# Strassen's algorithm on pairs of column tiles in three feed-forward products of a float32 kernel

## The chip, the cores and the metric

The kernel runs on one core of a Trainium2 chip. The metric is the device time of one execution in microseconds (us). All data are float32.

## The reference

Two transformer blocks run one after the other over 512 tokens of width 1024. The first is attention, convolution and gated linear attention, then a feed-forward network, then a per-layer gate. The second is a Fourier mixer beside an RWKV mixer, then a feed-forward network with a 3x3 convolution in its middle. What matters here are the two feed-forward networks, with 2816 hidden columns each:

```python
# first block
h = rms_norm(x, ffn_norm_g[i])
x = x + (jax.nn.silu(h @ ffn_w_gate[i]) * (h @ ffn_w_up[i])) @ ffn_w_down[i]
gate = jax.nn.sigmoid(rms_norm(x, ple_norm_g[i]) @ ple_w_gate[i])
x = x + (p[i] @ ple_w_proj[i]) * gate
...
# second block
x = x + g2 * conv_ffn(h, ffn_w_up[l], ffn_conv_w[l], ffn_conv_b[l], ffn_w_down[l], rows)
# conv_ffn: depthwise 3x3 convolution of h @ w_up, then (silu(gate) * val) @ w_down
```

## The kernel before

Activations lie transposed: 128 channels on the partitions, 512 tokens along the row. A weight matrix comes as a stream of **units** of 512 KB, each eight 128x128 tiles. A unit is the eight contraction tiles of one 128-column tile. SyncE loads the units in the order of `STREAM` into a ring of four slots and reloads a slot when `units_done` says that TensorE has finished with it. `product` (L330 is its matmul) multiplies the eight tiles of a unit with the eight token tiles of 512 columns and accumulates them in one PSUM bank.

Every engine has its own queue, written out by hand, stage after stage, and the engines meet only at semaphores. The parts that the change touches come in this order on TensorE:

- `out1` (L1205): eight units; VectorE adds each result to the residual stream `xT` (L1232).
- `norm_ffn`: ScalarE scales and squares each `xT` tile as it comes (L369, L370), GpSimd adds the squares (L386), TensorE sums over partitions with a matrix of ones (L394, L396), ScalarE takes the root (L374, L375, each behind a table load). It is folded: the products run on values that are not yet divided by the root, and VectorE multiplies the results by it.
- `ffn1` (L330): 22 pairs of a gate unit and an up unit. VectorE rescales both (L1314, L1316), ScalarE takes the silu (L1298), VectorE multiplies (L1319). Between the units lie 28 units of another product, `ada` (L1155), that is not part of the network.
- `ple_project` (L1345): two units, with ScalarE copying the results out (L1356).
- `down1` (L1205): 24 units, 22 contraction tiles for each of eight output tiles, with 12 more `ada` units between.
- `norm_ple` and `ple_gate` (L330 again): the same folded norm, and eight units.
- much later `ffn2` (L330): 44 units. ScalarE copies each result into a padded grid (L2547), VectorE applies nine taps to it (L2576, L2578), ScalarE takes the silu (L2554), VectorE multiplies (L2587).
- `down2` (L1205): 24 units, VectorE adding with a gate factor (L1234), then the last norm (L394, L396, L374, L375, L408) and the stores.

In `ffn2` and in a few other stages TensorE walks through its units in a hardware loop of four units; in `ffn1` and `down1` they are written out.

## Time and profile before

| what | value |
|---|---|
| median of three runs | 1976.53 us (1972.60 to 1979.27) |
| span of the profiled execution | 1970.1 us; its own time is not listed apart from these three |
| what lies around the span | 2.5 to 9.2 us by the three runs, 6.4 us by the median |
| TensorE busy | 1876.9 us, 95% of the span |
| VectorE, ScalarE, GpSimd busy | 770.6, 477.2, 237.2 us |
| mean granted TensorE clock | 0.985 |

The span runs from the first to the last instruction. Each matmul of the program shows as two rows of the trace, and so does each weight load, so a unit of eight matmuls is 16 rows.

### The profile page before, as it was taken

How to read it: one execution, taken by the hardware profiler on the slowest of the kernel's cores; microseconds unless marked ns; L12 is line 12 of the kernel's file. 1: busy time of each engine (PE TensorE's matmuls, PEld its weight loads, DVE VectorE, ACT ScalarE, POOL GpSimd, SP SyncE). 2: the span in 40 equal slices, each digit the busy share in tenths (PEclk: the TensorE clock that was granted, in tenths of full speed). 3: DMA queues.
4: the chain of work that ended last, by engine and by line, in shares of the span. 5: the costliest groups of instructions: out<-in, count | busy, mean ns of one | idle time of the engine just before them, and what ended most of it. 6: DMA issues, size and time to landing. Idle time of an engine off the chain costs nothing.

```text
span 1970.1 us, 33620 instructions
## 1 busy us (share of the span) xinstructions
PE 1876.9 (95%) x13862; PEld 995.4 (51%) x13862; DVE 770.6 (39%) x1560; ACT 477.2 (24%) x982; POOL 237.2 (12%) x284
## 2 busy tenths in 40 slices
PE   7999999999999999999999979888898999999997
PEld 3455774444444444434455448888743444444443
DVE  3551451011111100003332367666634888898001
ACT  3022562210000000033411554444412222221001
POOL 1140011000000000013000045555110000000000
PEclk9999998999999999999999989999999999999999
DMA  6421001333432223333311200000111222222222
GB/s 225 155 76 60 37 1 64 107 129 130 148 129 78 82 92 122 117 118 129 142 54 54 70 1 5 5 4 4 52 54 64 75 75 75 81 79 75 75 85 96
DMA packets 43862, 158.63 MB, mean 81 GB/s; under 512 B 5017, under 2 KB 5673, under 8 KB 42713
## 3 DMA queue, kind: packets, MB, share of 16 engines
q1 hardware_dynamic: 37440, 133.19, 20.0%
q10 hardware_dynamic: 6296, 23.58, 3.3%
q8 instruction: 102, 1.67, 0.4%
q14 instruction: 24, 0.19, 0.0%
HBM read 152.01 MB, written 6.31 MB: 80 GB/s over the span
## 4 chain that ended last, share of the span: by engine, by line
PE 88%; DVE 5%; ACT 4%; issue 1%; DMA 0%; POOL 0%; DVEq 0%; SPq 0%; ACTq 0%; POOLq 0%
PE psum L330 47%; PE psum L1205 21%; PE psum L1987 2%; PE psum L1991 2%; PE psum L995 1%; DVE mem L2177 1%; PE psum L588 1%; PE psum L1155 1%; PE psum L976 1%; PE psum L963 1%; PE psum L1753 1%; PE psum L631 1%; PE psum L1345 1%; PE psum L1998 1%; DVE mem L2205 1%
## 5 line engine op out<-in xcount | busy, mean ns | idle before, releaser
L330 PE MATMUL psum<-mem 128*128 128x512 f32 (+1 forms) x2272 | 961.5, 582 | 19.9 <-DMA mem<-in_units 11.7
L330 PEld LDWEIGHTS psum<-mem 128*128 128x128 f32 x2272 | 426.9, 190 | 525.0 <-issue 509.8
L1205 PE MATMUL psum<-mem 128*128 128x512 f32 x960 | 420.0, 596 | 4.1 <-DVE mem L2497 2.6
L1205 PEld LDWEIGHTS psum<-mem 128*128 128x128 f32 x960 | 181.3, 190 | 235.0 <-issue 227.3
L2578 DVE SCALAR_TENSOR_TENSOR mem<-mem 128x512 f32<-128x512 f32 x352 | 235.0, 744 | 0.0
L386 POOL TENSOR_TENSOR mem<-mem 128x512 f32<-128x512 f32 x24 | 30.5, 1270 | 1094.2 <-ACT mem L370 1093.8
L1987 PE MATMUL psum<-mem 64*64 64x64 f32 x1920 | 73.8, 222 | 12.1 <-DVE mem L2205 5.4
L1298 ACT ACTIVATE mem<-mem 128x512 f32<-128x512 f32 x22 | 13.9, 630 | 290.7 <-DVE mem L1314 290.6
L1234 DVE SCALAR_TENSOR_TENSOR mem<-psum,mem 128x512 f32 x16 | 12.0, 750 | 177.4 <-PE psum L1205 177.4
L1991 PE MATMUL psum<-mem 64*64 64x64 f32 x1920 | 71.4, 221 | 2.5 <-issue 2.0
L1987 PEld LDWEIGHTS psum<-mem 64*64 64x64 f32 x1920 | 64.7, 136 | 17.7 <-DVE mem L2205 10.9
L1316 DVE TENSOR_TENSOR mem<-psum,mem 128x512 f32<-128x512 f32 x22 | 15.2, 692 | 144.1 <-PE psum L330 144.1
L1225 DVE TENSOR_TENSOR mem<-mem,psum 128x512 f32<-128x512 f32 x8 | 5.5, 688 | 168.4 <-PE psum L1205 168.4
L1314 DVE TENSOR_TENSOR mem<-psum,mem 128x512 f32<-128x512 f32 x22 | 15.2, 692 | 138.8 <-PE psum L330 128.4
L2547 ACT COPY mem<-psum 128x512 f32<-128x512 f32 x44 | 25.8, 587 | 174.6 <-PE psum L330 174.5
L1991 PEld LDWEIGHTS psum<-mem 64*64 64x64 f32 x1920 | 64.0, 135 | 5.1 <-issue 3.3
L370 ACT ACTIVATE mem<-mem 128x512 f32<-128x512 f32 x32 | 19.9, 623 | 192.5 <-DVE mem L1234 192.5
L2294 ACT COPY mem<-psum 128x256 f32<-128x256 f32 x120 | 45.0, 375 | 88.2 <-PE psum L1987 86.7
L2204 DVE COPY_PREDICATED mem<-mem,psum 128x256 f32<-128x256 int32 x96 | 40.9, 426 | 35.3 <-PE psum L1991 35.2
L1035 DVE CUSTOM_DVE_ANT_0 mem<-psum,mem 128x512 f32<-128x512 f32 (+3 forms) x64 | 28.9, 489 | 46.2 <-PE psum L963 46.2
L2143 POOL TENSOR_TENSOR mem<-mem 128x256 f32<-128x256 f32 x12 | 12.0, 998 | 269.4 <-DVE mem L2160 269.4
L2205 DVE STREAM_TRANSPOSE mem<-mem 128x256 f32<-128x256 f32 x96 | 42.8, 446 | 3.3
(355 smaller groups left out, 1743.8 us busy)
## 6 DMA issues: line engine op xcount, KB each, us to landing
mem<-in_units SPq DMA_DIRECT2D x248, 512.0 KB, 3.4
mem<-in_cw ACTq DMA_DIRECT2D x2, 2048.0 KB, 10.4
mem<-in_wn ACTq DMA_DIRECT2D x1, 2048.0 KB, 8.6
bias_tiles<-bias_scratch ACTq DMA_DIRECT2D x1, 2048.0 KB
mem<-bias_tiles ACTq DMA_DIRECT2D x1, 2048.0 KB, 10.5
mem<-in_xT ACTq DMA_DIRECT2D x1, 2048.0 KB, 9.9
x_scratch<-mem ACTq DMA_DIRECT2D x1, 2048.0 KB, 8.7
mem<-x_scratch ACTq DMA_DIRECT2D x1, 2048.0 KB, 8.2
```

The costliest lines, as they stand in the source:

```text
L330: last = pe.matmul(dst, ring[:, slot, k, :], rhs(k), start=(k == 0), stop=(k == 7))
L370: eng.activation(sqr[:, k, 0:n], src(k), ACT.Square).then_inc(squared, 1)
L386: steps.link(eng.tensor_tensor(sqr[:, 0, 0:n], sqr[:, 0, 0:n], sqr[:, k, 0:n], ALU.add))
L1035: last = eng.tensor_tensor_reduce(sc[u % 2][g][:, 0:n], bank[:, 0:n], bias[:, h, 128 * (3 - i):512], -1.0, 1e20, ALU.add, ALU.min, low[u % ...
L1205: last = eng.matmul(ps[m % 4], ring[:, slot, k - 8 * part, :], rhs(k), start=(k == 0), stop=(k == ktiles - 1))
L1987: each(lambda hp, c, t: eng.matmul(dst(E_[d], hp, t), g[t, hp, 1, :], T[t, hp, :], start=True, stop=True)).then_inc(q["made"], 1)
L1991: each(lambda hp, c, t: eng.matmul(dst(O_[d], hp, t), a[t, hp, :], b_[t, hp, :], start=True, stop=True)).then_inc(q["made"], 1)
L2204: steps.link(eng.copy_predicated(split(T), bc22(kept), heads(O_[d])))
L2205: eng.transpose(flat(Tt), flat(T)).then_inc(q["grown"], 1)
L2294: eng.copy(split(s["Z"]), heads(E_[d])).then_inc(q["kept"], 1)
L2547: eng.copy(pad[:, j, 1:9, 1:65], ps[j].rearrange("p (y x) -> p y x", y=8)).then_inc(padded, 1)
L2578: steps.did_but(1, lambda: eng.scalar_tensor_tensor(cacc[:, j], src, w, cacc[:, j], ALU.mult, ALU.add))
```

## The change

`ffn1`, `down1` and `down2` no longer multiply one column tile at a time. They take **two column tiles at once**, halve the contraction and the tokens (512 into 256 and 256), and form the 2x2 block product with seven half-width products instead of eight, in the variant of the algorithm that shares sums. A product of `ffn1` has four contraction tiles (`half`), one of `down1` and `down2` has eleven, taken in chunks of four, four and three (`CHUNKS`, `part`).

- **Weight sums.** VectorE forms four sums of weight tiles for each pair of units, `lay_weights` and `lay_last_weights`, each 128x512 (128x384 for the last chunk): 22 times in `ffn1`, 12 times in each `down`. The pair of units for the next step is summed during the current one.
- **Token sums.** For `ffn1` VectorE forms them tile by tile behind `out1` (`lay_tokens`: one operation of 128x256 for each of the first four tiles, three for each of the last four). For `down1` and `down2` GpSimd forms them (`lay_products`), four operations of 128x256 for each of 11 pairs of hidden tiles.
- **PSUM partial results.** In `ffn1` ScalarE copies one bank out three times in a step (`head`, `mid`, `tail`), because four products accumulate in it one behind the other, and VectorE adds these copies to two other banks. The order on TensorE in step n is p11(n), p22(n-1), the `ada` units, s1(n), s4(n-1), s2(n), p12(n), s3(n). In the `down` products 11 half-width VectorE operations for each pair of output tiles take the place of two full-width ones, and ScalarE copies one half bank.
- **Order.** `ple_project` moves from before `down1` to after it, its two units on either side of the norm's sum; the norms take their tiles in the order 0, 4, 1, 5, 2, 6, 3, 7. The `ada` units are grouped: two in each of the first six steps, one in each of the other 16.
- **Ring and loops.** From `ffn1` to `ple` the ring has six slots. TensorE's and SyncE's loops over units are written out everywhere.

```diff
-STREAM = [("in1", 17), ("out1", 8), ("ffn1", 2 * FT + 28), ("pleproj", 2), ("down1", 36),
+STREAM = [("in1", 17), ("out1", 8), ("ffn1", 2 * FT + 28), ("down1", 36), ("pleproj", 2),
           ("ple", 16), ("in2", 19), ("out2", 8), ("ffn2", 2 * FT), ("down2", 24)]
+WIDE = ("ffn1", "down1", "pleproj", "ple")
+NSLOTS, NWIDE = 4, 6
...
+    for _ in range(_c):
+        _s = min(range(NWIDE if _n in WIDE else NSLOTS), key=lambda k: _last[k])
+        _turns[_s] += 1
+        SLOT.append(_s)
+        TURN.append(_turns[_s])
...
+        _last[_s] = NUNITS
+        NUNITS += 1
+HALF = FT // 2
+CHUNKS = [(0, 4), (4, 8), (8, 11)]
...
+        def lay_weights(eng, done, base, w1, w2, to, nk):
+            at = (slice(None), slice(0, nk), slice(None))
+            hi = (slice(None), slice(4, 4 + nk), slice(None))
+            eng.tensor_tensor(to[:, 0][at], w2[at], w2[hi], ALU.add).then_inc(done, 1)
+            eng.tensor_tensor(to[:, 2][at], w1[at], w2[at], ALU.subtract).then_inc(done, 1)
+            eng.wait_ge(done, base + 1)
+            eng.tensor_tensor(to[:, 1][at], to[:, 0][at], w1[at], ALU.subtract).then_inc(done, 1)
...
+            at = (slice(None), slice(0, nk), slice(None))
+            eng.wait_ge(done, base + 3)
+            eng.tensor_tensor(to[:, 3][at], w1[:, 4:4 + nk, :], to[:, 1][at], ALU.subtract).then_inc(done, 1)
...
+        def lay_products(eng, base, lo, hi, to):
+            eng.tensor_tensor(to[:, 0], lo[:, CTX:S], lo[:, 0:CTX], ALU.subtract).then_inc(act_laid, 1)
+            eng.wait_ge(act_laid, base + 1)
+            eng.tensor_tensor(to[:, 1], hi[:, CTX:S], to[:, 0], ALU.subtract).then_inc(act_laid, 1)
+            eng.tensor_tensor(lo[:, CTX:S], hi[:, CTX:S], lo[:, CTX:S], ALU.subtract).then_inc(act_laid, 1)
+            eng.wait_ge(act_laid, base + 2)
+            eng.tensor_tensor(to[:, 2], hi[:, 0:CTX], to[:, 1], ALU.subtract).then_inc(act_laid, 1)
...
+                def half(dst, w, rhs, start=True, stop=True, before=None):
+                    for k in range(4):
+                        if before:
+                            before(k)
+                        last = eng.matmul(dst, w[:, k, :], rhs(k), start=start and k == 0, stop=stop and k == 3,
+                                          skip_group_check=True)
+                    return last
...
+                for n in range(FT):
+                    p11(n)
+                    if n:
+                        p22(n - 1)
+                    else:
+                        s1(n)
+                        sums(eng, steps)
+                        eng.wait_ge(cond, 1)
+                    ada_units(eng, sum(ADA1[:n]), ADA1[n])
+                    if n == 6:
                         ctx_sum(eng)
+                    if n:
+                        s1(n)
+                        s4(n - 1)
+                    s2(n)
+                    p12(n)
+                    s3(n)
+                p22(FT - 1)
+                s4(FT - 1)
...
+                    eng.wait_ge(made, after("11", n))
+                    if n:
+                        eng.wait_ge(taken, 4 * (n - 1) + 1)
+                    eng.copy(head, bank_y(n)).then_inc(kept, 1)
...
+                    eng.wait_ge(made, after("s2", n))
+                    if n:
+                        eng.wait_ge(taken, 4 * (n - 1) + 4)
+                    eng.copy(mid, bank_y(n)).then_inc(kept, 1)
+                    if n % 2:
+                        q = n // 2
+                        for side in (1, 0):
+                            eng.wait_ge(taken, 4 * (n - 1) + 3)
+                            eng.wait_ge(scaled, 2 * n - side)
+                            g = actT[:, q + HALF * side, :]
+                            eng.activation(g, g, ACT.Silu).then_inc(silued, 1)
+                    eng.wait_ge(units_done, pair_unit(n) + 1)
+                    if n:
+                        eng.wait_ge(taken, 4 * (n - 1) + 2)
+                    eng.copy(tail, bank_y(n)).then_inc(kept, 1)
...
+                    if n:
+                        eng.wait_ge(kept, 3 * m + 3)
+                        eng.wait_ge(made, after("s1", m))
+                        eng.tensor_tensor(place(m, 1)[:, CTX:S], bank_z(m), tail, ALU.add).then_inc(taken, 1)
+                        eng.wait_ge(units_done, pair_unit(m) + 2)
+                        if m == 0:
+                            rooted(eng)
+                        eng.tensor_tensor(place(m, 1)[:, 0:CTX], bank_y(m), rstd[:, 0:CTX], ALU.mult).then_inc(taken, 1)
+                        scale(place(m, 1)[:, CTX:S], rstd[:, CTX:S], m, 4 * m + 2)
+                        if n == FT:
+                            down1_first[0](eng)
+                        eng.wait_ge(made, after("s4", m))
+                        eng.tensor_tensor(place(m, 0)[:, CTX:S], bank_z(m), mid, ALU.add).then_inc(taken, 1)
+                        scale(place(m, 0), rstd, m, 4 * m + 4)
+                    if n + 1 < FT:
+                        pair_sums(eng, n + 1)
+                        pair_last_sum(eng, n + 1)
+                    if n and m % 2:
+                        q = m // 2
+                        eng.wait_ge(taken, 4 * m + 3)
+                        for side in (1, 0):
+                            eng.wait_ge(silued, 2 * q + 2 - side)
+                            eng.wait_ge(scaled, 2 * m + 2 - side)
+                            g = actT[:, q + HALF * side, :]
+                            eng.tensor_tensor(g, g, upT[:, side, :], ALU.mult).then_inc(multiplied, 1)
...
+                    if n < FT:
+                        eng.wait_ge(made, after("12", n))
+                        eng.wait_ge(kept, 3 * n + 1)
+                        eng.tensor_tensor(place(n, 0)[:, 0:CTX], bank_x, head, ALU.add).then_inc(taken, 1)
+            def pool(eng, steps):
+                for q in range(HALF):
+                    eng.wait_ge(multiplied, 2 * q + 2)
+                    lay_products(eng, 4 * q, actT[:, q, :], actT[:, q + HALF, :], actX[:, :, q, :])
...
+                        return ins
+                    def freed(count):
...
+                    if between:
+                        between(eng, j)
+                    if m == 0:
+                        eng.wait_ge(act_laid, laid + 4 * k1)
+                    unit_landed(eng, u)
+                    freed(2)
+                    if first and m:
+                        eng.wait_ge(kept, r + m)
+                    part(a[:, lo], held(u), lambda k: low(k)[:, lo], True, False)
+                    ins = part(a[:, hi], held(u)[:, 4:8], lambda k: high(k)[:, lo], False, True)
+                    if last_:
+                        ins.then_inc(made, 1)
+                    freed(4)
+                    eng.wait_ge(summed, s0 + 4 * j + 3)
+                    part(b[:, lo], to[:, 1], lambda k: extras[:, 1, k, :], True, False)
+                    ins = part(b[:, hi], to[:, 2], lambda k: low(k)[:, hi], False, True)
+                    if last_:
+                        ins.then_inc(made, 1)
+                    freed(10)
+                    eng.wait_ge(summed, s0 + 4 * j + 4)
+                    part(c[:, lo], to[:, 0], lambda k: extras[:, 0, k, :], True, False).then_inc(units_done, 1)
+                    ins = part(c[:, hi], to[:, 3], lambda k: high(k)[:, hi], False, True)
+                    if last_:
+                        ins.then_inc(made, 1)
+                    freed(11)
+                    unit_landed(eng, u + 1)
+                    part(d[:, lo], held(u + 1)[:, 4:8], lambda k: extras[:, 2, k, :], True, True).then_inc(units_done, 1)
...
+                        weights(eng, j + 1)
+                        continue
+                    m = j // 3
+                    t = 11 * (r + m)
+                    x, y = xT[:, m, :], xT[:, m + 4, :]
+                    eng.wait_ge(made, 3 * (r + m) + 1)
+                    eng.wait_ge(kept, r + m + 1)
+                    add(x[:, lo], a[:, lo], m)
+                    eng.wait_ge(taken, t + 1)
+                    add(x[:, lo], a[:, hi], m)
+                    if j < 11:
+                        weights(eng, j + 1)
+                    eng.wait_ge(made, 3 * (r + m) + 2)
+                    eng.tensor_tensor(u2, b[:, lo], p1, ALU.add).then_inc(taken, 1)
+                    eng.wait_ge(taken, t + 3)
+                    eng.tensor_tensor(u3, b[:, hi], u2, ALU.add).then_inc(taken, 1)
+                    add(x[:, hi], u2, m)
+                    eng.wait_ge(taken, t + 4)
+                    add(y[:, hi], u3, m + 4)
+                    add(y[:, lo], u3, m + 4)
+                    eng.wait_ge(made, 3 * (r + m) + 3)
+                    eng.wait_ge(taken, t + 5)
+                    add(x[:, hi], c[:, lo], m)
+                    eng.wait_ge(taken, t + 6)
+                    add(y[:, hi], c[:, lo], m + 4)
+                    eng.wait_ge(taken, t + 8)
...
+        def ple_project():
+            u0 = UNIT0["pleproj"]
...
+                    return last
+                per_unit(eng, u0, 1, lambda w, j: use(w, 0))
+                folds[-1][0](eng, None)
+                per_unit(eng, u0 + 1, 1, lambda w, j: use(w, 1))
...
-                eng.dma_start(ring[:, j], units[j]).then_inc(landed[j], 16)
-            with eng.Fori(1, nunits // 4) as i:
-                for j in range(4):
-                    eng.wait_ge(units_done, 4 * i + (j - 3))
-                    eng.dma_start(ring[:, j], units[4 * i + j]).then_inc(landed[j], 16)
+            for n in range(1, NUNITS):
+                if n == UNIT0["ffn1"]:
+                    eng.wait_ge(stage_done, 4)
+                if FREED[n]:
+                    eng.wait_ge(units_done, FREED[n])
```

## Rows read from the trace of the kernel before

**Rows 1.** Page, busy time and share of each engine, and the granted clock by slice.

```profile
PE 1876.9 (95%) x13862; PEld 995.4 (51%) x13862; DVE 770.6 (39%) x1560; ACT 477.2 (24%) x982; POOL 237.2 (12%) x284
...
PEclk9999998999999999999999989999999999999999
```

**Rows 2.** Page, shares of the chain that ended last.

```profile
PE 88%; DVE 5%; ACT 4%; issue 1%; DMA 0%; POOL 0%; DVEq 0%; SPq 0%; ACTq 0%; POOLq 0%
```

**Rows 3.** Chain of waits at the start of ffn1 (start, us, what, rows of it).

```profile
364.41 6.87 PE psum L330 x16
...
373.00 0.57 PE psum L1155 x16
373.57 7.07 PE psum L330 x16
...
411.78 3.65 PE psum L1145 x16
```

**Rows 4.** Groups by form, in2's first stretch: count | busy, mean ns.

```profile
L330 PE MATMUL psum<-mem 128*128 128x256 f32 x160 | 36.2, 378 | 0.0
```

**Rows 5.** Chain of waits over the same stretch.

```profile
953.12 130.81 PE psum L330 x384
```

**Rows 6.** Groups by form, whole run: scalar, vector, GpSimd and narrow matmuls.

```profile
L2294 ACT COPY mem<-psum 128x256 f32<-128x256 f32 x120 | 45.0, 375 | 88.2 <-PE psum L1987 86.7
...
L1319 DVE TENSOR_TENSOR mem<-mem 128x512 f32<-128x512 f32 x22 | 15.2, 693 | 0.8
...
L2371 POOL TENSOR_TENSOR mem<-mem 128x256 f32<-128x256 f32 x22 | 14.2, 646 | 0.0
...
L631 PE MATMUL psum<-mem 128*128 128x62 f32 x128 | 14.5, 274 | 0.0
```

**Rows 7.** Chain of waits between ffn1 and down1.

```profile
693.52 6.89 PE psum L1345 x16
...
701.16 7.12 PE psum L1345 x16
```

**Rows 8.** Chain of waits between down1 and the gate product.

```profile
868.12 0.62 PE psum L1155 x16
...
878.14 1.27 POOL mem L386
...
880.70 0.86 PE psum L396 x2
881.55 0.65 PE psum L1166 x6
...
882.78 13.94 PE psum L330 x32
```

**Rows 9.** Chain of waits, whole run: ffn2, then down2.

```profile
1499.44 290.80 PE psum L330 x672
1804.74 151.61 PE psum L1205 x352
```

**Rows 10.** Timeline of VectorE at the end of ffn2.

```profile
1804.72 0.88 DVE L2576 TENSOR_SCALAR mem<-mem 128x512 f32<-128x512 f32 x2 [0.75 <-ACT mem L2547]
...
1817.58 0.75 DVE L2587 SCALAR_TENSOR_TENSOR mem<-mem 128x512 f32<-128x512 f32 x1 [0.26 <-DVE mem L2587]
```

**Rows 11.** Timeline of TensorE over the same change of stage.

```profile
1804.74 7.55 PE L1205 MATMUL psum<-mem 128*128 128x512 f32 x17 [0.77 <-DVEq L2602]
```

**Rows 12.** Groups by form, VectorE in ffn2.

```profile
L2576 DVE TENSOR_SCALAR mem<-mem 128x512 f32<-128x512 f32 x42 | 18.6, 485 | 28.9 <-ACT mem L2547 28.9
```

**Rows 13.** One VectorE line with both inputs in SBUF (min/median/max ns).

```profile
L2226 DVE TENSOR_TENSOR mem<-mem x22: 411/424/986, 1192.4 to 1404.2; 128x256 f32<-128x256 f32 x22
```

**Rows 14.** Timeline of ScalarE behind the sum of squares in ffn1.

```profile
373.04 0.69 ACT L374 ACTIVATE mem<-psum,mem 128x512 f32<-128x512 f32 x1 [5.19 <-PE psum L396]
...
375.04 0.63 ACT L375 ACTIVATE mem<-mem 128x512 f32<-128x512 f32 x1
```

**Rows 15.** Timeline of the run's end.

```profile
1956.63 0.75 DVE L1234 SCALAR_TENSOR_TENSOR mem<-psum,mem 128x512 f32 x1 [4.41 <-PE psum L1205]
```

More of the change, by code:

```diff
@@ L346, in norm @@
         def norm(src, dst, g, n=S, shift=None, source=None, pooled=True, before_sum=None, after_sum=None,
-                 rows=None, late_rows=None, columns=None, folded=False):
+                 rows=None, late_rows=None, columns=None, folded=False, order=range(KT)):
             squared, added, summed, rooted, scaled, shifted = norm_sems
@@ L364, in act @@
                     eng.wait_ge(sem("eps_set"), 1)
-                for k in range(KT):
+                for k in order:
                     if source:
@@ L1125, in ada_unit @@
         def ada_unit(n):
-            return UNIT0["ffn1"] + 2 * n + 1 if n < 28 else UNIT0["down1"] + 3 * (n - 28) + 2 if n < 40 else \
-                UNIT0["ple"] + (1, 4, 5, 7, 9, 11, 13, 15)[n - 40]
+            if n < 28:
+                step = next(k for k in range(FT) if sum(ADA1[:k + 1]) > n)
+                return pair_unit(step) - sum(ADA1[:step + 1]) + n
+            return UNIT0["down1"] + 3 * (n - 28) if n < 40 else UNIT0["ple"] + (1, 4, 5, 7, 9, 11, 13, 15)[n - 40]
         def ada_bank(b):
@@ L1186, in ctx_root, with residual @@
             eng.wait_ge(ctx_summed, 1)
-            eng.tensor_scalar(rstdc2, ps[6][:, 0:CTX], 1.0 / D, EPS, ALU.mult, ALU.add).then_inc(ctx_varied, 1)
-        def residual(tag, rhs, ktiles=8, gate=None, ready=None, primed=False, before=None, extra=None):
+            eng.tensor_scalar(rstdc2, ps[7][:, 0:CTX], 1.0 / D, EPS, ALU.mult, ALU.add).then_inc(ctx_varied, 1)
+        def residual(tag, rhs, ktiles=8, gate=None, ready=None, primed=False, before=None, after=None):
             free = sem("residual_free")
@@ new lines, in before, with added @@
+            def before(eng):
+                eng.wait_ge(sem("f1_taken"), 4 * (FT - 1) + 1)
+            pe, dve, copy, source, weights = paired_residual(
+                "down1", 3, lambda k: actT[:, k, :], lambda k: actT[:, HALF + k, :], actX, 0, wsum, [hX[2][:, k, :] for k in range(3)], (0, 2, 7, 6), before, between)
+            down1_first.append(lambda eng: weights(eng, 0))
+            def added(eng, k):
+                if 1 <= k <= 3:
+                    ada_row(eng, 6 + k)
+                if k < 4:
+                    copy(eng, k)
+                source(eng, k)
@@ L1411, in unit, with use @@
                 def unit(m):
[L1412 removed]
+                    def use(slot, j):
                         if m >= 4:
@@ L2526, in build @@
         csil = r11.take(2, S)
+        act2X = r11.take(3, HALF, CTX)
+        wsum2 = r11.take(2, 4, 4, P)
+        down2_work = [r11.take(CTX) for _ in range(3)]
+        down2_first, down2_added = [], []
         fcw = cols[:, COL0["fc_w"]:COL0["fc_w"] + 396].rearrange("p (k t) -> p k t", k=9)
@@ L2712, in pairs @@
         return np.stack([_tiles(a), _tiles(b)], axis=1).reshape(-1, P, 8, P)
-    units["ffn1"] = pairs(g["ffn_w_gate"][0], g["ffn_w_up"][0])
-    units["down1"] = _thirds_last(_tiles(g["ffn_w_down"][0]))
+    sides = _tiles(g["ffn_w_gate"][0]), _tiles(g["ffn_w_up"][0])
+    units["down1"] = _paired(g["ffn_w_down"][0], range(FT))
     pp = g["ple_w_proj"][0].reshape(2, P, 2, 4, P).transpose(2, 1, 3, 0, 4).reshape(2, P, 8, P)
```

482 lines of the change are left out of this document (294 added, 188 removed).

## The prediction

> **What bounds the kernel now.** I read the page's busy shares first: TensorE is busy for 95% of the span, VectorE for 39% [rows 1]. A busy TensorE can still be one that waits inside a matmul, so I read the chain of waits next: 88% of what ended last is TensorE [rows 2], at its full clock in nearly every slice [rows 1]. In the three changed parts the chain is nothing but matmuls: a unit of `ffn1` is 16 rows in 6.87 us, 0.4294 us a row [rows 3], and `down2` is 352 rows in 151.61 us [rows 9]. So fewer TensorE columns shorten the run one for one, as long as two things hold: a half-width row costs half, and the extra work of VectorE, ScalarE and GpSimd stays beside it.
>
> **Price of a half-width row.** The stretch of `in2` shows both kinds: 384 rows in 130.81 us, of which 160 are 256 wide [rows 4, 5]. The 224 wide ones take 224 x 0.4294 = 96.2 us; the rest, 34.6 us over 160, is 0.2165 us a row, each with its own weight load. The sum of squares in `ffn1` gives 3.65 / 16 = 0.228 with the switch to it [rows 3], and the busy time of the group 36.2 / 160 = 0.226 [rows 4]. I take 0.2165 and keep 0.226 as the upper bound; a matmul 62 columns wide is busy for 14.5 / 128 = 0.113 us a row [rows 6], so the weight load alone needs no more than that.
>
> **TensorE, part by part.**
> - `ffn1`: 44 units x 16 = 704 rows go, 302.3 us. 22 pairs x 7 products x 4 matmuls x 2 = 1232 half rows come, 266.7 us. Gain 35.6.
> - `down1`, `down2`: 352 rows (151.1 us) each against 4 x 7 x 11 x 2 = 616 half rows (133.4 us). Gain 17.7 each, 35.5 together.
> - `ada` units in groups: the first unit behind one takes 7.07 instead of 6.87 [rows 3], so a switch costs 0.20; six fewer, gain 1.2.
> - `ple_project` behind `down1`: the pause in its middle goes (693.52 + 6.89 to 701.16, 0.75 us [rows 7]). From the end of `down1`'s last `ada` unit (868.74) to the second gate unit's stretch (882.78) 14.04 us pass for 6.87 + 2 x 0.86 + 0.65 + 0.57 = 9.81 us of work [rows 8]: the gate's first unit waits for ScalarE tile by tile, and the sum for GpSimd. Now 6.9 us of `ple_project` lie there first, and the other 6.9 us cover the root. Gain 4.2 + 0.75 = 5.0.
> - Loops written out: `ffn2`'s rows go at 290.80 / 672 = 0.4327 [rows 9], `ffn1`'s, already written out, at 0.4294: 704 x 0.0033 = 2.3, and 0.5 in `down2` (151.61 - 151.1). Gain 2.8, if fetching the longer program costs nothing; nothing bounds it but this.
> - `down2` no longer waits for the last copy of `ffn2` (its first matmul starts at 1804.74 after 0.77 us idle [rows 11], so `ffn2` ended at 1803.97): gain 0.8.
>
> Sum of gains: 80.9 us.
>
> **Beside TensorE.** A step of `ffn1` is now 28 x 2 x 0.2165 = 12.1 us and 0.57 + 0.2 for `ada`, 12.9 us. VectorE does in it four sums of 128x512 at 0.69, one rescaling at 0.69, two products every second step (0.69 a step), and five operations of 128x256 at some 0.42 [rows 6, 13]: 6.2 us, 48%. ScalarE does three copies at 0.375 [rows 6] and a silu. GpSimd has four operations of 0.646 every second step [rows 6]. The order matters more than the sum: p22 needs the copy `tail` of what s3 left, and only p11 (1.73 us) stands between them; the copy takes 0.375 and the two hand-overs 0.1 to 0.3 each (the last one of the run: end 1956.35, VectorE starts 1956.63 [rows 9, 15]), so about 1 us is left. The copy `mid` has p12 between s2 and s3, the same. s4 of the step before needs one add, three products ahead. The weight sums of step n+1 are done about 11 us into step n and are first read 4 us into the next. I cost the steady steps at nothing; without this cover each 1 us would be 22 us. In a `down`, 33.3 us of TensorE for a pair of output tiles stand against 7.7 us of weight sums and 11 adds of some 0.42: hidden. The units come at the same size with six slots, and no load sets the pace.
>
> **What is not hidden.**
> - *Start of `ffn1`.* `head` of step 0 stands on ScalarE behind the root: from 373.00, when the sum ends, to the end of the second activation at 375.04 + 0.63 = 375.67 [rows 3, 14], then the issue of the `pT` load and the copy, about 3.2 us. TensorE has two `ada` units, 1.3 us. s2(0) waits 1.9 us (0 to 3).
> - *`ffn2` into `down2`.* VectorE is the late one: it ends at 1817.58 + 0.75 = 1818.33 [rows 10]. Four weight sums (2.8 us) are put ahead of its last taps, where it idles 0.75 [rows 10]: it ends 2.0 later, at 1820.4. Behind that stand the sums of chunk 1, three of which (2.1 us) TensorE needs: 1822.5. TensorE is there at 1804.0 + 12.1 + 3.5 = 1819.6. A wait of 2.9 us. GpSimd's token sums for the last two pairs fall into the same stretch. Both engines read two SBUF operands there, and a VectorE operation of 0.424 took up to 0.986 [rows 13]. I take 0.2 each for eight, so 4.5 in all (2.9, to 2.9 + 8 x 0.56 = 7.4).
> - *`ffn2` itself.* VectorE idles 28.9 us there for want of input [rows 12]. 44 GpSimd operations that each held it for 0.56 would cost 24.7, still under that. Hidden; without cover up to 10.
> - *The end.* The last two tiles now finish together (3 and 7). Tile 3 needs its square and a GpSimd add of 1.27 [rows 8] before the first sum matmul, which stood ready before. By that chain the root starts some 4.3 us behind the last product instead of 3.0: 1.4 us (1 to 2).
>
> Losses: 1.9 + 4.5 + 1.4 = 7.8 us. Net gain 80.9 - 7.8 = 73.1 us: the span would be 1897.0, and the median of runs, 6.4 above the span, 1903.4.
>
> **The skill against a row.** One VectorE operation took 0.986 instead of 0.424 while GpSimd was at work [rows 13]; GpSimd's own take 0.646 [rows 6]. The Trainium skill, "SBUF — State Buffer", section "Who interferes with whom", says the two share one port pair that is locked for a whole instruction when both read two SBUF operands. By it each of the last eight token sums would hold VectorE for its full 0.646, and the wait at `down2` would come to an estimated 8 us instead of 4.5, the result near 1907.
>
> **Rivals.**
> - *A. The hand-over chain of `ffn1` shows.* For: four products wait for one bank's copies within a step, each with about 1 us of room, and ScalarE and VectorE work strictly in order, so a silu or a multiply ahead of a copy makes it late. Against: the sums above. At 1 us a step it costs 22 us: 1925; with the same in the 24 chunks of the `down`s 1950.
> - *B. VectorE and GpSimd block each other so that `ffn2` turns VectorE-bound.* For: rows 13. Against: 28.9 us idle [rows 12]. If each GpSimd operation cost VectorE a full 0.99, 44 of them would be 43.6, 14.7 over: 1918.
> - *C. Slower than before: half-width rows don't cost half.* For: a weight load goes with every 256 columns instead of every 512, from weights that VectorE has just written. Against: 0.2165 in `in2`, with a load each. The break-even is 0.2165 + 73.1 / 2464 = 0.246 us a row. With half of the 0.113 us of a load and its narrow matmul exposed [rows 6], 0.056 more a row, 2464 rows lose 138 us and the run is 138 - 73 = 65 us slower: 2042. On a page: the Trainium skill, "TensorE: Matmul & The Clock Gate", section "Back-to-back issue gap", gives sustained spacings of about 81 ns at 128 columns and 131 ns at 512; a straight line between them puts 256 columns at 0.75 of 512, which would be an estimated 0.32 us a row here and some 250 us lost. The trace disagrees: 0.2165 against 0.4294 is 0.504 [rows 3 to 5].
>
> **How the numbers follow.** My forecast, with waits between none and all bounds above, holds 0.76; within it 1893 (no stall at all, the lowest run) to 1913 (0.226 a row costs 23 us, of which I keep a part, and the longer waits). A holds 0.14, B 0.05, C 0.03, and 0.02 is left for something that cancels the gain. The median of such a kernel can tell 0.3%, 6 us, from no change. The range runs from 1893 to 1924: it takes in the near half of A and most of B. Faster by over 0.3%: 0.95; within: 0.02; slower: 0.03.
>
> **What would show it.** In the profile after: `ffn1`'s steps 12.9 us apart with no idle TensorE ahead of p22 or s3; 616 half rows of each `down` in 133 us; a single wait near 2 us at s2(0) and one of 3 to 7 us in `down2`'s second chunk, on VectorE; no wait between `down1` and `in2`'s start that wasn't there before. It is wrong if the half rows are spaced above 0.22, if VectorE or ScalarE ends regular waits in `ffn1`, or if the written-out queues leave gaps that nothing explains.

## The result and the profile after

The changed kernel takes 1916.71 us (median of 4 runs, 1913.45 to 1917.94) against 1974.57 (4 runs, 1967.02 to 1979.27): a ratio of 0.9701, interval 0.9675 to 0.9728. The profiled execution spans 1914.5 us, 55.6 less than before; 73.1 less were forecast. The time is 13.3 us above the forecast of 1903.4 and inside its range of 1893 to 1924.

The page after. VectorE went from 39% [rows 1] to 50%. It is busy for 80% and more in slices 32 to 37, which are `ffn2`, and 3 to 4 tenths behind them, in `down2`:

```profile
PE 1811.7 (95%) x14918; PEld 1202.8 (63%) x14918; DVE 960.1 (50%) x1920; ACT 502.0 (26%) x1056; POOL 306.4 (16%) x372
...
DVE  3560442334444423233231577666615899899433
...
PE 75%; DVE 10%; issue 9%; ACT 3%; DVEq 1%; DMA 0%; POOL 0%; SPq 0%; ACTq 0%; POOLq 0%
...
L1557 PE MATMUL psum<-mem 128*128 128x256 f32 x1232 | 274.3, 383 | 11.7 <-DVE mem L1297 11.7
L1382 PE MATMUL psum<-mem 128*128 128x256 f32 x1232 | 274.2, 382 | 2.5 <-issue 2.5
```

On the chain TensorE fell from 88% [rows 2] to 75%. VectorE has 10%, and most of the 9% "issue" is the gaps between VectorE's own operations in `ffn2`. The two groups of half rows say where to look: `ffn1` (L1382) waited 2.5 us in all, the `down`s (L1557) 11.7 us, and VectorE's weight sums (L1297) ended that.

Next the chain of waits (start, length, what), steady steps first, then the two places where TensorE stood:

```profile
371.07 2.01 issue
373.08 10.57 PE psum L1382 x40
...
467.16 12.30 PE psum L1382 x56
480.04 12.31 PE psum L1382 x56
...
673.98 12.30 PE psum L1557 x56
...
1780.03 118.28 PE psum L1557 x538
```

A run of 56 half rows takes 12.30 us with 0.20 for the switch to it: (12.30 - 0.20) / 56 = 0.216 us a row, in `ffn1` and in `down1` (a half row is a row of the trace 256 columns wide). The steps of `ffn1` with one `ada` unit are 12.88 us apart (480.04 - 467.16). Right behind the 2.01 us at s2(0) stand 40 rows in 10.57 us, 1.9 more than 40 x 0.2165 = 8.66. The timeline has the waits of `down2` and the last product:

```profile
1749.98 3.62 PE L1557 MATMUL psum<-mem 128*128 128x256 f32 x16
1761.97 14.72 PE L1557 MATMUL psum<-mem 128*128 128x256 f32 x56 [8.37 <-DVE mem L1297]
1780.03 45.19 PE L1557 MATMUL psum<-mem 128*128 128x256 f32 x200 [3.34 <-DVE mem L1297]
...
1895.75 3.84 PE L1557 MATMUL psum<-mem 128*128 128x256 f32 x17
...
1901.77 1.13 PE L427 MATMUL psum<-mem 128*128 128x512 f32 x2 [2.18 <-POOLq L420]
...
1903.80 0.69 ACT L407 ACTIVATE mem<-psum,mem 128x512 f32<-128x512 f32 x1 [1.72 <-PE psum L429]
```

A chunk of four contraction tiles is 56 half rows. So the first wait, 8.37 us, stands behind the first 16 half rows of `down2`, inside its first chunk; the second, 3.34 us, stands 56 rows later, at the same place of the second chunk. The forecast had a wait in the second chunk alone. The 56 rows between the two take 14.72 us instead of 56 x 0.2165 = 12.1. The table sets stretches side by side (us), by the starts of their first matmuls (the last product ends at 1895.75 + 3.84 = 1899.59):

| stretch | before | after | change | forecast |
|---|---|---|---|---|
| start to `ffn1` | 364.41 | 364.88 | +0.5 | 0 |
| `ffn1` | 329.11 | 295.65 | -33.5 | -34.9 |
| `down1`, to the second gate unit | 189.26 | 165.99 | -23.3 | -22.7 |
| gate, to `in2`'s long stretch | 70.34 | 72.04 | +1.7 | 0 |
| `in2` to `ffn2` | 546.32 | 547.18 | +0.9 | 0 |
| `ffn2` and `down2`, to the last product | 456.91 | 453.85 | -3.1 | -16.8 |
| the end | 13.75 | 14.91 | +1.2 | +1.4 |

So `down1` and the end came as worked out, and `ffn1` to 1.4 us. Of the 17.5 us missing, 13.7 are in `ffn2` and `down2`, and the rest lies in small pieces of 0.5 to 1.7 us in four other stretches.

### The profile page after: what moved, and what is told of

Read it like the earlier page. It is cut to its first block, busy times and chain, and to the rows that moved or that the text cites. A ratio compares the mean times of both kernels' runs of the same rounds, so it can differ in the third digit from the quotient of the medians.

```text
span 1914.5 us, 35490 instructions
## 1 busy us (share of the span) xinstructions
PE 1811.7 (95%) x14918; PEld 1202.8 (63%) x14918; DVE 960.1 (50%) x1920; ACT 502.0 (26%) x1056; POOL 306.4 (16%) x372
## 4 chain that ended last, share of the span: by engine, by line
PE 75%; DVE 10%; issue 9%; ACT 3%; DVEq 1%; DMA 0%; POOL 0%; SPq 0%; ACTq 0%; POOLq 0%
PE psum L364 21%; PE psum L1382 14%; PE psum L1557 13%; PE psum L1242 6%; DVE mem L2908 4%; PE psum L2313 2%; PE psum L2317 2%; PE psum L1029 2%; DVE mem L2503 1%; PE psum L622 1%; PE psum L1010 1%; PE psum L1191 1%; PE psum L997 1%; PE psum L2079 1%; DVE mem L2916 1%
## 5 line engine op out<-in xcount | busy, mean ns | idle before, releaser
L364 PE MATMUL psum<-mem 128*128 128x512 f32 (+1 forms) x1568 | 652.1, 576 | 17.9 <-DMA mem<-in_units 10.8
L364 PEld LDWEIGHTS psum<-mem 128*128 128x128 f32 x1568 | 297.6, 191 | 361.1 <-issue 342.2
L1557 PE MATMUL psum<-mem 128*128 128x256 f32 x1232 | 274.3, 383 | 11.7 <-DVE mem L1297 11.7
L1382 PE MATMUL psum<-mem 128*128 128x256 f32 x1232 | 274.2, 382 | 2.5 <-issue 2.5
L1557 PEld LDWEIGHTS psum<-mem 128*128 128x128 f32 x1232 | 234.5, 191 | 49.3 <-DVE mem L1297 12.5
L1382 PEld LDWEIGHTS psum<-mem 128*128 128x128 f32 x1232 | 232.1, 190 | 40.5 <-issue 7.6
L2908 DVE SCALAR_TENSOR_TENSOR mem<-mem 128x512 f32<-128x512 f32 x352 | 239.3, 755 | 0.0
L1242 PE MATMUL psum<-mem 128*128 128x512 f32 x256 | 114.1, 606 | 3.1 <-DVEq L2825 1.9
L1309 POOL TENSOR_TENSOR mem<-mem 128x256 f32<-128x256 f32 x22 | 16.4, 745 | 582.3 <-DVE mem L2916 308.2
L1242 PEld LDWEIGHTS psum<-mem 128*128 128x128 f32 x256 | 49.2, 194 | 67.4 <-issue 62.1
L1294 DVE TENSOR_TENSOR mem<-mem 128x512 f32<-128x512 f32 (+1 forms) x46 | 32.4, 703 | 99.9 <-DMA mem<-in_units 82.0
L2620 ACT COPY mem<-psum 128x256 f32<-128x256 f32 x120 | 45.0, 375 | 90.0 <-PE psum L2313 89.0
L2469 POOL TENSOR_TENSOR mem<-mem 128x256 f32<-128x256 f32 x12 | 12.0, 998 | 271.1 <-DVE mem L2486 271.1
L1069 DVE CUSTOM_DVE_ANT_0 mem<-psum,mem 128x512 f32<-128x512 f32 (+3 forms) x64 | 28.9, 489 | 46.8 <-PE psum L997 46.8
L1463 ACT COPY mem<-psum 128x256 f32<-128x256 f32 x22 | 8.2, 372 | 159.5 <-PE psum L1382 159.5
```

The source lines that it names most:

```text
L364: last = pe.matmul(dst, w[:, k, :], rhs(k), start=(k == 0), stop=(k == 7))
L1242: last = eng.matmul(ps[m % 4], w[:, k - 8 * part, :], rhs(k), start=(k == 0), stop=(k == ktiles - 1))
L1294: eng.tensor_tensor(to[:, 0][at], w2[at], w2[hi], ALU.add).then_inc(done, 1)
L1382: last = eng.matmul(dst, w[:, k, :], rhs(k), start=start and k == 0, stop=stop and k == 3, skip_group_check=True)
L1557: ins = eng.matmul(dst, w[:, k, :], rhs(k0 + k), start=opens and first and k == 0, stop=closes and last_ and k == k1 - k0 - 1, skip_group_ ...
L2620: eng.copy(split(s["Z"]), heads(E_[d])).then_inc(q["kept"], 1)
```

## Why down2 waits longer: VectorE in ffn2

VectorE's timeline in the middle of `ffn2` (start, busy, what, idle before): two taps with a scalar, 16 taps, the product that makes a row of `act2T`; a half step with GpSimd's sums beside it, then one without:

```profile
1643.92 0.75 DVE L2916 SCALAR_TENSOR_TENSOR mem<-mem 128x512 f32 x1 [0.55 <-DVE mem L2908]
1645.53 1.91 DVE L2906 TENSOR_SCALAR mem<-mem 128x512 f32<-128x512 f32 x2 [0.85 <-DVE mem L2916]
1647.36 11.15 DVE L2908 SCALAR_TENSOR_TENSOR mem<-mem 128x512 f32<-128x512 f32 x16
...
1660.29 0.88 DVE L2906 TENSOR_SCALAR mem<-mem 128x512 f32<-128x512 f32 x2 [0.47 <-DVE mem L2916]
1661.08 10.69 DVE L2908 SCALAR_TENSOR_TENSOR mem<-mem 128x512 f32<-128x512 f32 x16
1672.32 0.75 DVE L2916 SCALAR_TENSOR_TENSOR mem<-mem 128x512 f32 x1 [0.55 <-DVE mem L2908]
```

The four GpSimd sums cost VectorE 1.03 us on the scalar taps and 0.46 on the others: 1.5 us, 0.37 for each. A double step is 1672.32 - 1643.92 = 28.40 us. Before, with the first two half steps of `ffn2` ahead:

```profile
1516.07 0.88 DVE L2576 TENSOR_SCALAR mem<-mem 128x512 f32<-128x512 f32 x2 [10.13 <-ACT mem L2547]
...
1529.95 0.88 DVE L2576 TENSOR_SCALAR mem<-mem 128x512 f32<-128x512 f32 x2 [2.39 <-ACT mem L2547]
...
1542.08 0.75 DVE L2587 SCALAR_TENSOR_TENSOR mem<-mem 128x512 f32 x1 [0.65 <-DVE mem L2578]
1543.69 0.88 DVE L2576 TENSOR_SCALAR mem<-mem 128x512 f32<-128x512 f32 x2 [0.86 <-ACT mem L2547]
...
1569.61 0.75 DVE L2587 SCALAR_TENSOR_TENSOR mem<-mem 128x512 f32 x1 [0.65 <-DVE mem L2578]
```

There a double step is 1569.61 - 1542.08 = 27.5 us, TensorE's pace (64 rows). In after the releaser of L2906 is no longer ScalarE's copy of TensorE's output but VectorE's own product: VectorE sets its own pace and falls 0.9 us behind in each double step. TensorE does not feel it inside `ffn2`; the lag is handed over at its end. TensorE leaves `ffn2` at 1750.15. In the kernel before, VectorE finished its last row but two of `act2T` at the moment when TensorE left `ffn2` (both at 1803.97); here it finishes that row 8.1 us later, at 1758.29. Only then come the weight sums of `down2`'s first chunk, and with GpSimd's sums beside them they take 0.97 to 1.21 us instead of 0.69:

```profile
1757.54 0.75 DVE L2916 SCALAR_TENSOR_TENSOR mem<-mem 128x512 f32 x1 [0.55 <-DVE mem L2908]
1758.68 0.97 DVE L1294 TENSOR_TENSOR mem<-mem 128x512 f32<-128x512 f32 x1 [0.39 <-DVE mem L2916]
1759.57 1.21 DVE L1295 TENSOR_TENSOR mem<-mem 128x512 f32<-128x512 f32 x1
```

TensorE, in its first chunk, waits for the third of these (L1297), to 1761.97. The forecast had these sums ready in time, and without the lag they are: in e2 below there is no wait in the first chunk. The sums of the second chunk stand behind VectorE's last row, as forecast, and end the second wait. That one is 3.34 us, near the 2.9 that the forecast worked out from the weight sums alone, because by then the first wait had made TensorE as late as VectorE.

## Experiments

All ratios are to the kernel before on the same chip: 1971.14 us (9 runs) for e1 to e4, 1973.16 (11 runs) for e5 to e8. "After" is the changed kernel. The start of `ffn1` shifts by up to 8 us from one profiled execution to another (359.57 to 367.66), ahead of everything that these edits change, so spans are compared from there on: after has 1914.5 - 364.88 = 1549.6. Several expectations compare whole spans and carry that shift with them. Line numbers are each kernel's own.

### e1_plain_down2: Strassen in ffn1 and down1 only

```diff
-                down2_first[0](eng)
+                eng.sem_inc(sem("residual_free"), 4)
...
-            pe, dve, copy, source, weights = paired_residual("down2", ...)
+            return residual("down2", lambda k: act2T[:, k, :], ktiles=FT, ..., ready=ready, primed=True)
...
-    units["down2"] = _paired(g["ffn_w_down_2"][0], ...)
+    units["down2"] = _thirds_last(_tiles(g["ffn_w_down_2"][0]))
```

> The changed kernel with down2 alone as it was before: eight full-width tiles, no GpSimd work in ffn2, the last norm in its old order. My theory is that the half-width products of down2 save 17.7 us of TensorE rows and lose nearly all of it to waits on VectorE, to the lower clock behind these waits, and to a longer end. From the start of ffn2 to the end of the span the changed kernel takes 468.8 us and the kernel before 470.7 us, so I expect a span of about 1916.4 us (1914 to 1919), the same as the changed kernel's 1914.5 within 0.3%. The rival, that down2's part of the saving is there and the missing time was lost elsewhere, expects some 13 us more: a span of 1927 us.

1915.62 us (1911.61 to 1919.22, 5 runs), ratio 0.9719 [0.9702, 0.9735]; after has 0.9701 [0.9675, 0.9728]. The chain has all of `down2` in one piece:

```profile
1748.71 151.61 PE psum L1242 x352
```

From `ffn2`'s start (1443.52) to the last product (1900.32) 456.8 us pass, and 13.5 to the end: 470.3, against 453.85 + 14.91 = 468.8 in after. Strassen in `down2` is worth 1.5 us of the 17.7 that it takes off TensorE. In the medians it does not show. The rival, some 13 us more, is ruled out. The old product with its loop written out takes the same 151.61 us as before [rows 9].

### e2_no_token_sums: GpSimd does nothing in ffn2

```diff
+                eng.wait_ge(used_dve, 2)
+                eng.memset(act2X, 0.0).then_inc(sem("act2x_set"), 1)
+                eng.wait_ge(sem("act2x_set"), 1)
                 for i in range(NI):
                     eng.wait_ge(used_dve, 2 * i + 2)
-                    lay_products(eng, 4 * (HALF + i), act2T[:, 2 * i, :], act2T[:, 2 * i + 1, :], act2X[:, :, i, :])
+                    eng.sem_inc(act_laid, 4)
```

> The changed kernel without GpSimd's 44 token sums during ffn2 (left out: the three extra token operands of down2 hold zeros and the second token half is not rewritten; all matmuls and all VectorE work stay). Theory A: VectorE falls 8 us behind in ffn2 because GpSimd's two-operand work holds up its own, so without it a double step takes the 27.5 us of TensorE again instead of 28.4, the weight sums at the end of ffn2 take 0.69 us each instead of 1.13, the wait of down2 falls from 11.7 to about 3 us, and one of two periods at the lower clock (about 2.3 us) goes too: span about 1903 us. Theory B, that the place of the weight sums in VectorE's queue alone makes the wait: only the shorter sums help, some 3 us: span about 1911 us.

1904.94 us (1903.44 to 1908.08, 5 runs), ratio 0.9663 [0.965, 0.9676]; 1538.8 us from `ffn1`'s start, 10.8 less than after. VectorE's timeline again:

```profile
1642.40 0.75 DVE L2916 SCALAR_TENSOR_TENSOR mem<-mem 128x512 f32 x1 [0.55 <-DVE mem L2908]
...
1669.30 0.75 DVE L2916 SCALAR_TENSOR_TENSOR mem<-mem 128x512 f32 x1 [0.55 <-DVE mem L2908]
```

A double step is 26.90 us, so VectorE has 27.5 - 26.9 = 0.6 us to spare in each, and GpSimd takes 1.5. That it goes below the 27.5 of the expectation has a cause in the edit: the one GpSimd operation that is left, the memset, held VectorE up by 6.91 - 0.88 = 6.0 us near the start of `ffn2`, and VectorE made up 0.6 us of that in each double step:

```profile
1502.55 7.14 POOL L2938 MEMSET mem<- 128x8448 f32 x1 [68.13 <-DVE mem L2916]
1503.44 6.91 DVE L2906 TENSOR_SCALAR mem<-mem 128x512 f32<-128x512 f32 x2 [0.95 <-ACT mem L2877]
```

The waits of `down2`:

```profile
PE psum L1557 <- DVE mem L1297: 3.7, 1, 3.7
```

One wait of 3.7 us stays, in the second chunk, where the prediction had worked out 2.9 from the weight sums alone. The other 0.8 is what is left of the memset's delay (VectorE ends that row at 1750.75, TensorE `ffn2` at 1749.99). The first chunk's wait is gone. So at least 8.0 of the 11.7 us come from GpSimd's token sums.

### e8_double: GpSimd's work in ffn2 doubled

```diff
+                        for x in range(4):
+                            eng.tensor_tensor(spare, act2T[:, 2 * i, CTX:S], act2T[:, 2 * i + 1, 0:CTX],
+                                              ALU.subtract).then_inc(sem("spare"), 1)
```

> The changed kernel with GpSimd's work during ffn2 doubled: four more operations of 128x256 with two SBUF operands for each of the first ten pairs, written to a spare tile that nobody reads. In the changed kernel four such operations lengthen VectorE's double step from 27.5 to 28.4 us while 0.9 us of its idle time goes too, so they cost it some 1.5 us. If each operation costs VectorE the same, the double step becomes 29.9 to 30.5 us, VectorE falls behind by some 2.7 us in each of ten, TensorE has to wait inside ffn2 itself once a few units are stored up, and the span grows by 15 to 22 us: 1930 to 1937 us. If the contention has no part in the lag, the span stays at 1914.5 us.

1935.06 us (1931.29 to 1942.35, 4 runs), ratio 0.9814 [0.9786, 0.9842]; 1569.4 us from `ffn1`'s start, 19.8 more than after. Timeline and waits:

```profile
1652.21 0.75 DVE L2917 SCALAR_TENSOR_TENSOR mem<-mem 128x512 f32 x1 [0.55 <-DVE mem L2909]
...
1682.49 0.75 DVE L2917 SCALAR_TENSOR_TENSOR mem<-mem 128x512 f32 x1 [0.55 <-DVE mem L2909]
```

```profile
PE psum L1557 <- DVE mem L1297: 30.5, 2, 25.4
```

A double step is 30.28 us, 1.88 more; ten of them make 18.8, and TensorE's waits grew from 11.7 to 30.5, by 18.8. The expectation had TensorE waiting inside `ffn2`; it still waits nowhere there. With e2 these are three doses of GpSimd work, none, one and two (26.90, 28.40, 30.28 us): what exceeds 27.5 is paid at `down2`, once for each double step. By the double steps that should be 10 x 0.9 = 9 and 10 x 2.78 = 28 us; over e2's wait without the memset's share (3.7 - 0.8) the waits are 8.8 and 27.6 us longer.

### e3_early_weights: down2's first weight sums taken out of the stretch

The first four units of `down2` are loaded during `ffn2` into a tile that stands empty, and the weight sums of its first two chunks are made at the start of `ffn2`, where VectorE has nothing to do.

```diff
+                down2_first[0](eng)
                 taps(0, 0)
...
-                down2_first[0](eng)
                 taps(NI - 1, 1)
...
-            down2_first.append(lambda eng: weights(eng, 0))
+            down2_first.append(lambda eng: [weights(eng, j) for j in range(2)])
...
+                if n == UNIT0["ffn2"] + 4:
+                    eng.wait_ge(norm_sems[2], squares_read[0])
+                    for i in range(EARLY):
+                        eng.dma_start(held(UNIT0["down2"] + i), units[UNIT0["down2"] + i]).then_inc(sem("early"), 16)
```

> The changed kernel with down2's first four units loaded at the start of ffn2 into memory that is free then, and the weight sums of its first two chunks formed there, where VectorE waits 10 us for its first input. Nothing else is changed; GpSimd's token sums stay. If the wait of down2 is for these sums, its 11.7 us go and with them about 4.3 us at the lower clock; the next thing late is GpSimd's last token sums (VectorE ends ffn2 near 1772, GpSimd near 1776, the third chunk begins near 1775), 0 to 1.5 us. Span about 1900 us (1898 to 1903). The rival, that VectorE's lag of 8 us is passed on to whatever comes next, expects a wait of 6 to 8 us in the third chunk and a span near 1908 us.

1900.64 us (1898.51 to 1906.18, 5 runs), ratio 0.9648 [0.9632, 0.9663]; 1537.1 us from `ffn1`'s start, 12.5 less than after. All the waiting in `down2`:

```profile
PE psum L1569 <- POOL mem L1326: 3.2, 1, 3.2
```

VectorE is still 8 us late at the end of `ffn2`, but the first thing that TensorE needs from behind this lag is now the last pair's rows, in the third chunk. The 11.7 us became 3.2 us there, on GpSimd's sums of that pair; the rival had 6 to 8. The profiled span is 1896.7, but 5.3 us of its distance to after's 1914.5 are an earlier start of `ffn1`; the gain behind that start is 12.5 us where about 14.5 were expected.

### e6_last_pair: e3, and the last pair of ffn2 read without its token sums first

```diff
-                        eng.wait_ge(act_laid, laid + 4 * k1)
+                        if ungated:
+                            eng.wait_ge(ungated, 2 * k1)
...
+                    if m == 0:
+                        eng.wait_ge(act_laid, laid + 4 * k1)
...
+                eng.wait_ge(act_laid, 4 * (HALF + NI - 1))
+                lay_products(eng, 4 * (HALF + NI - 1), act2T[:, FT - 2, :], act2T[:, FT - 1, :], act2X[:, :, NI - 1, :])
...
-                for i in range(NI):
+                for i in range(NI - 1):
```

> The kernel with the early weight sums (e3), and the token sums of the last pair of hidden tiles on VectorE instead of GpSimd, at the end of its work in ffn2; the third chunk's first product, which reads no token sum, waits only for the gated tiles. In e3 TensorE waits 3.2 us there for GpSimd's last sum and runs some 1.7 us longer at the lower clock. If only that sum is late, both go: 4.9 us, span 1892 us. If VectorE's lag of 8 us is itself the limit, a wait of 1 to 3 us stays at the second product: span 1894 to 1896 us.

1900.92 us (1895.53 to 1903.07, 5 runs), ratio 0.9628 [0.9606, 0.965]; 1535.3 us from `ffn1`'s start. The ratio is not told from e3's 0.9648 by its interval, so the times do not show a gain. The span of 1892 us did not come: it is 1899.1. The chain:

```profile
1749.21 26.80 PE psum L1569 x124
1776.03 105.32 PE psum L1569 x486
...
1884.83 1.84 PE psum L439 x2
```

No wait is left: 610 half rows in 132.1 us, 0.2166 each. So the half rows of `down2` cost what those of `ffn1` do once nothing stands before them. `down2` itself is 4.7 us shorter than in e3 (1743.63 to 1881.78 there, 1749.21 to 1882.64 here), near the 4.9 forecast. From `ffn1`'s start the total gained only 1.8. The last line has about half of the reason: the end has a wait of 2.2 us on GpSimd, and in this execution the sum matmuls behind it ran at half clock (1.84 instead of 1.13), so the end takes 1899.1 - 1882.6 = 16.5 us instead of 14.9. The other 1.3 us lie ahead of `down2`, in code that e3 and e6 share. The expectation also started from e3's whole span, in which `ffn1` happened to start 4.2 us earlier than here.

### e5_tail: the last two tiles squared without GpSimd's add

```diff
-                    eng.wait_ge(squared, KT * r + KT)
-                    last = eng.matmul(ps[7][:, 0:n], ones, sqr[:, KT - 1, 0:n], start=False, stop=True)
+                    for k in range(KT - direct, KT):
+                        eng.wait_ge(squared, KT * r + k + 1)
+                        last = eng.matmul(ps[bank][:, 0:n], ones, sqr[:, order[k], 0:n], start=False, stop=(k == KT - 1))
...
-                        order=PAIRED)
+                        order=PAIRED, direct=2, bank=0)
```

> The changed kernel with the last norm's sum taken differently: GpSimd adds one tile fewer, TensorE sums the last two tiles (3 and 7) directly, in a bank that is free. In the changed kernel the first sum matmul waits 2.2 us for GpSimd's add of tile 3, and the root starts 5.5 us behind the last product. If the longer end comes from that add, the root starts some 2 us sooner: 1.3 us of add and 0.8 of hand-overs and waiting go, 0.86 of a matmul comes but mostly ahead of the last square. Span 1912.6 us (1912 to 1913.5). The rival, that the end is set by VectorE's last four additions, expects no change beyond 0.3 us.

1912.27 us (1909.01 to 1920.92, 6 runs), ratio 0.9695 [0.9672, 0.9718]: not told from after's by its interval. The chain tells more:

```profile
1904.49 0.86 PE psum L427 x2
...
1907.24 0.69 ACT mem L407
```

The root starts 2.75 us behind the last product (1904.49) instead of 4.2 (the expectation's 5.5 is no distance to the last product), and the end takes 13.5 us instead of 14.9. That agrees with the theory and not with the rival, in one profile. That this execution's span is 3.5 us above after's has another place: `in2` to `ffn2` took 552.7 us instead of 547.2, with 52.35 us for 114 rows of the same `out2` (49.29 at full clock), in code that the edit does not touch.

### e4_head_early: the copy of step 0 ahead of the root

```diff
+        def head_copy(eng):
+            eng.wait_ge(norm_sems[1], norms_added[0])
+            eng.wait_ge(sem("f1_made"), 1)
+            eng.copy(head, ps[0][:, 0:CTX]).then_inc(sem("f1_kept"), 1)
...
-                                       source=added(), folded=True)
+                                       source=added(), folded=True, rows=head_copy)
```

> The changed kernel with the first copy out of PSUM in ffn1 (head of step 0) put ahead of the root on ScalarE, so that s2(0) finds it done. The wait of 2.0 us at s2(0) goes. In the changed kernel TensorE's granted clock is 0.5 for some 3.5 us behind that wait, and the next 40 rows take 10.57 us instead of 8.66. If the lower clock comes from the wait, it goes too: 3.9 us, span 1910.6 us. If the clock falls anyway, only 2.0 us: span 1912.5 us.

1914.98 us (1906.79 to 1916.99, 5 runs), ratio 0.9705 [0.9685, 0.9726]; 1545.1 us from `ffn1`'s start, 4.5 less than after. The windows, first of after (us, busy times and counts, the granted clock, DMA share, GB/s), then of this kernel:

```profile
373.00:375.00 2.00, 1.92 (x7) 1.67 (x8) 0.00 (x0) 0.00 (x0) 0.00 (x0) 0.78 0.96 363
375.00:377.00 2.00, 2.00 (x6) 1.55 (x6) 0.00 (x0) 0.37 (x1) 0.00 (x0) 0.50 0.69 281
```

```profile
373.00:375.00 2.00, 2.00 (x11) 1.75 (x10) 0.00 (x0) 1.54 (x3) 0.00 (x0) 1.00 0.93 293
375.00:377.00 2.00, 2.00 (x11) 1.75 (x10) 0.00 (x0) 0.00 (x0) 0.00 (x0) 1.00 0.96 387
```

Without the wait there is no fall of the clock, with the same transfers running (0.93 and 0.96 of the DMA engines). So the lower clock comes from the wait: the wait of 2.0 us costs 3.9, itself and 1.9 us behind it. From `ffn1`'s start to the end of these 40 rows this profile takes 15.0 us instead of 18.8. Five runs do not resolve a gain of this size: the ratio is not told from after's.

### e7_all: e4, e5 and e6 together

```diff
-                                       source=added(), folded=True)
+                                       source=added(), folded=True, rows=head_copy)
...
-                        order=PAIRED)
+                        order=PAIRED, direct=2, bank=0)
...
+                        if ungated:
+                            eng.wait_ge(ungated, 2 * k1)
```

> The early copy of ffn1 (e4), the early weight sums with the last pair on VectorE (e6) and the shorter end (e5) together. If the three are independent, the gains add: from the changed kernel's 1914.5 us 3.9, 22.7 and 1.9 us go, span about 1886 to 1888 us, time 1889 to 1891. If a lower clock appears at another place of its own accord, up to 3 us more.

1890.01 us (1889.21 to 1901.51, 5 runs), ratio 0.9585 [0.9565, 0.9606], the fastest kernel of this study. The median is inside the forecast, and that is in part luck: of the 28.5 us added up there some 5 are the earlier start of `ffn1` in e3's profile. The profiled execution is the slowest of the five; it has 1532.0 us from `ffn1`'s start, 17.6 less than after, and 3.6 us more than after between `in2` and `ffn2`, where the two do not differ. The stage in question, and the first sum matmul behind it:

```profile
1752.83 26.80 PE psum L1577 x124
1779.65 106.61 PE psum L1577 x492
1886.26 0.86 PE psum L439 x2
```

616 half rows in 133.4 us, the prediction's number for a `down` to the tenth, and an end of 1899.7 - 1886.3 = 13.4 us.

## Why the prediction was right, and where not

The time lies inside the range, and the gains on TensorE came nearly as added up, those of the loops apart. But one term that the prediction put at nothing, VectorE's lag in `ffn2`, makes most of the miss, and another error hides a part of it.

- *From span to time.* The prediction added 6.4 us for what lies around the span, the difference between the median of three runs and the span of another execution. In every execution with both numbers listed, the time is 1.7 to 1.9 us above its own span (after: 1916.31 against 1914.5). With 1.8 the forecast would have been 1898.8 us. So 4.6 of the 17.5 us missing in the span do not show in the 13.3 us, by luck.
- *Price of a half-width row, and rival C.* Right: 0.216 us in all three parts.
- *`ffn1`, steady steps, and rival A.* Right: 12.88 us apart, and no wait ahead of p22 or s3. The room in the hand-overs, about 1 us, was enough.
- *`down1` and `ple_project`.* Right: 23.3 us against 22.7.
- *Start of `ffn1`.* The wait was 2.0 us for 1.9; the 1.9 us of lower clock behind it was in no term.
- *Loops written out, 2.3 us in `ffn2`.* Wrong. The 704 rows took 304.40 us against 304.53. The excess of 2.2 us over 0.4294 us a row is the clock at the start of `ffn2`, which is as low in both kernels (granted 0.58 over the first 4.3 to 4.6 us), behind a wait of 4.4 us on ScalarE. First before, then after:

```profile
1500.00:1502.00 2.00, 2.00 (x3) 0.67 (x2) 2.00 (x4) 2.00 (x4) 0.00 (x0) 0.50 0.00 0
```

```profile
1446.00:1448.00 2.00, 2.00 (x3) 0.89 (x4) 2.00 (x4) 2.00 (x4) 0.00 (x0) 0.50 0.03 8
```

- *`ffn2` itself, "Hidden".* This is the step that failed. The prediction set 28.9 us of VectorE's idle time [rows 12] against 44 operations. But 12.5 us of that idle lay before the first two half steps (10.13 and 2.39), and of the 0.86 us in each of the others 0.47 remains when VectorE is the bound, in its own hand-over. What could be used was 0.6 us a double step, some 6 in all, against 1.5 x 10 = 15 of slowing. The text's own reserve, "without cover up to 10", was near the 8.1 us that came. Rival B had the mechanism, VectorE as the bound of `ffn2`, with too high a price for each operation (0.99 us, measured 0.37). That the time came so close to its 1918 is chance: the lag explains 7.2 us of waits and 4.3 us at the lower clock, the rest of the distance is made of other terms.
- *`ffn2` into `down2`, 4.5 us.* It measured 11.7, because the step above fed it: 8.37 us in the first chunk, where the prediction had none, and 3.34 in the second, where it had its single wait. Another 4.3 us came at the lower clock (1899.59 - 1750.15 = 149.4 us for `down2`, less 133.4 for its rows and 11.7). Together 7.2 + 4.3 + 2.2 for the loops = 13.7 us, which is the shortfall of that stretch.
- *The end, 1.4 us.* Right: 1.2, with the root 4.2 us behind the last product (4.3 said).
- *The port.* The Trainium skill, "SBUF — State Buffer", section "Who interferes with whom", says that a GpSimd instruction that gets the shared ports first blocks VectorE for the whole of it. The runs agree that the two hinder each other. The memset of e2 agrees in size too: 7.14 us long, it held VectorE up by 6.0. The token sums do not: the first of the four ran in VectorE's own gap, and the other three, 0.73 to 0.91 us long, cost it 1.5 us together, 0.5 each. In e8 seven of eight stand beside it, 0.82 to 1.17 us long, and cost 30.28 - 26.90 = 3.4 us, 0.48 each. That it is a port that makes them hinder each other, no run here shows.

```profile
1644.75 0.73 POOL L1309 TENSOR_TENSOR mem<-mem 128x256 f32<-128x256 f32 x1 [25.13 <-DVE mem L2916]
```

- Left over is 1.7 us in the gate stretch: the same wait of 2.63 us is followed by rows at half clock in after (8.80 us for 16) and at full clock in before (7.11). What decides that is open.
- Moving all token sums of `ffn2` off GpSimd was not tried; e6 moved those of one pair of eleven.

## What to carry to other kernels

Idle time of an engine is no reserve until it is split: subtract what stands before the loop starts, and the hand-over that stays when that engine is the bound; compare the shortest possible step with the pace of the engine that leads. An engine that is slower than TensorE by 3% in a long stage shows no wait there, but all of it at the stage's end, so look for who must catch up at the next change of stage. To the price of a TensorE wait of 2 us or more add some 2 us for the clock behind it (1.9, 1.7 and 2.6 us behind waits of 2.0, 3.3 and 8.4 here; behind 2.2 and 2.6 us it came in some executions and not in others). And take what lies around the span from an execution that has both numbers.

## What the runs showed of the hardware

TensorE's granted clock fell to half (1.2 GHz) right behind short waits within dense work, for some 3 to 5 us. Windows of after behind the 8.37 us wait:

```profile
1762.00:1764.00 2.00, 2.00 (x5) 1.64 (x6) 2.00 (x4) 0.00 (x0) 0.49 (x1) 0.50 0.00 0
1764.00:1766.00 2.00, 2.00 (x7) 1.55 (x6) 2.00 (x4) 0.00 (x0) 0.00 (x0) 0.50 0.04 8
1766.00:1768.00 2.00, 2.00 (x9) 1.71 (x8) 2.00 (x4) 0.00 (x0) 0.00 (x0) 0.81 0.00 0
```

It fell behind waits of 2.0 us (s2(0), 10.56 or 10.57 us for 40 rows in after, e1, e2, e3, e5, e6 and e8), 3.3, 4.4 and 8.4 us, and not behind 0.77 us [rows 11]. Waits of 2.2 and 2.6 us went both ways (the end of e6 and of after, the gate of after and of before). While it is down a row costs about double: over some 5 us at half clock behind the 8.37 us wait the 56 half rows took 2.6 us longer.
